# Compressing the sample's cached rows by three block products per pair of blocks instead of four

## What is computed

```python
def _compress(kv, pe, w1, w2):
    # block i covers positions [i*16, i*16 + 32); pe (2, 32, 64); w1 (2, 32, 64, 128); w2 (2, 128, 64)
    ch = kv[:, :n * CMP_STRIDE].reshape(B, n, CMP_STRIDE, 2, K, Dh)
    parts = []
    for half in range(r):                       # r = 2
        sl = slice(half * CMP_STRIDE, (half + 1) * CMP_STRIDE)
        pe_h = jnp.moveaxis(pe[:, sl], 0, 1)[:, :, None]
        proj = jnp.einsum('bncskd,scdh->bnskh', ch + pe_h, w1[:, sl])
        parts.append(proj[:, half:half + n_cmp])
    hid = jax.nn.silu(sum(parts))
    return jnp.einsum('bnskh,shd->bnskd', hid, w2)
```

## Time and profile before

| | us |
|---|---|
| median of 3 runs | 2289.65 (2289.12 to 2290.79) |
| the profiled execution | 2288.92 |
| its span, first to last instruction | 2287.1 |

### The profile page before, as it was taken

One profiled execution on the slowest core, in us unless ns is written; L12 is line 12 of the kernel. 1 busy time (PEld: TensorE's weight loads), 2 busy tenths in 40 slices (PEclk: granted clock), 3 DMA queues, 4 the chain that ended last, 5 costly groups with the idle time before them and its releaser, 6 DMA issues.

```text
span 2287.1 us, 42944 instructions
## 1 busy us (share of the span) xinstructions
PE 2191.5 (96%) x13416; PEld 1569.2 (69%) x13416; DVE 893.4 (39%) x2336; ACT 564.1 (25%) x1372; POOL 646.6 (28%) x733
## 2 busy tenths in 40 slices
PE   7999998999999999999999999989999999999997
PEld 4545567677777777777745556767777677777776
DVE  2013763433453222336510147533344523133475
ACT  2111661211113322120211146411111233121202
POOL 0001771101143334434200037510113334333440
PEclk9999999999999999999999999999999999999999
DMA  9733026999964444544275310389999444444441
GB/s 347 255 148 92 7 78 190 277 277 276 274 231 167 172 172 182 198 190 183 106 276 202 141 61 0 105 264 278 275 284 301 179 155 188 172 172 172 177 166 42
DMA packets 130750, 424.93 MB, mean 186 GB/s; under 512 B 18337, under 2 KB 90274, under 8 KB 114082
## 3 DMA queue, kind: packets, MB, share of 16 engines
q1 hardware_dynamic: 108928, 326.01, 40.2%
q10 hardware_dynamic: 21666, 97.06, 14.6%
HBM read 412.40 MB, written 152.57 MB: 247 GB/s over the span
## 4 chain that ended last, share of the span: by engine, by line
PE 86%; issue 4%; DVE 4%; SPq 1%; POOL 1%; DMA 1%; ACT 1%; DVEq 0%; POOLq 0%; ACTq 0%
PE bank L1099 39%; PE bank L1182 14%; PE bank L1395 10%; PE bank L1568 2%; PE bank L1362 2%; PE bank L1330 2%; PE bank L1342 2%; PE bank L1464 2%; PE bank L1195 1%; PE bank L1592 1%; POOL zone L945 1%; PE bank L1519 1%; DMA ring<-in_cache_kv_cmp 1%; PE bank L1540 1%; SPq L514 1%
## 5 line engine op out<-in xcount | busy, mean ns | idle before, releaser
L1099 PE MATMUL bank<-zone,ring 128*128 128x288 f32 x1664 | 424.8, 407 | 10.3 <-DVE zone L1730 7.6
L1099 PEld LDWEIGHTS bank<-zone,ring 128*128 128x128 f32 x1664 | 314.8, 190 | 103.3 <-DVE zone L1730 13.1
L1099 PE MATMUL bank<-zone,w 128*128 128x288 f32 x1408 | 353.5, 406 | 0.0
L1182 PE MATMUL bank<-ring,hT 128*128 128x512 f32 (+2 forms) x800 | 329.7, 566 | 6.2 <-ACTq L767 4.9
L1099 PEld LDWEIGHTS bank<-zone,w 128*128 128x128 f32 x1408 | 267.5, 190 | 73.9
L1182 PEld LDWEIGHTS bank<-ring,hT 128*128 128x128 f32 (+1 forms) x800 | 147.4, 189 | 157.6 <-issue 146.6
L1395 PE MATMUL bank<-ring,w 128*128 128x128 f32 x2048 | 245.2, 279 | 10.4 <-DMA ring<-in_cache_kv_cmp 10.4
L899 POOL TENSOR_TENSOR w<-ring 128x512 f32<-128x512 f32 x72 | 93.5, 1299 | 546.3 <-PE bank L1099 309.3
L1395 PEld LDWEIGHTS bank<-ring,w 128*128 128x128 f32 x2048 | 235.5, 194 | 14.6 <-DMA ring<-in_cache_kv_cmp 10.5
L629 ACT COPY zone<-bank 128x288 f32<-128x288 f32 x72 | 28.6, 398 | 557.5 <-PE bank L1099 557.5
L1021 POOL TENSOR_TENSOR zone<-constants,stat 128x1024 f32<-128x1024 f32 x16 | 30.3, 1897 | 427.2 <-DVE stat L2089 427.2
(11 more groups left out here) (251 smaller groups left out, 2681.1 us busy)
## 6 DMA issues: line engine op xcount, KB each, us to landing
out_dil_s<-in_state_kv_dil SPq DMA_DIRECT2D x48, 2720.0 KB, 12.3
ring<-in_w_units SPq DMA_DIRECT2D x72, 1024.0 KB, 4.8
ring<-in_cache_kv_cmp SPq DMA_DIRECT2D x256, 128.0 KB, 3.1
ring<-in_cache_kv_sel SPq DMA_DIRECT2D x256, 128.0 KB, 9.9
zone<-in_batch_rows ACTq DMA_DIRECT2D x14, 2112.0 KB
zone<-in_batch_rows ACTq DMA_DIRECT2D x30, 768.0 KB, 5.6
ring<-in_w_in SPq DMA_DIRECT2D x10, 2048.0 KB, 8.1
zone<-in_batch_rows ACTq DMA_DIRECT2D x14, 1088.0 KB, 6.3
```

The costliest lines, as they stand in the source:

```text
L1099: last = mm(dst[:, 0:HALF], lhs[:, k, :], rhs(k), start=first and k == 0, stop=(k == 3), skip_group_check=True)
L1182: last = mm(dst, hT[:, k, t * P:t * P + ROWS[t]], ring[:, n % 2, k * CH:k * CH + width], start=start and k == 0, stop=stop and k == KT - 1)
```

## The change

Neighbouring chunks are treated in pairs, an even one e and an odd one o. Three products are made of each pair in place of four: B·e (`second_of_even`), A·o (`first_of_odd`), and (A + B)·(e + o) (`both_of_sum`). Token e, which is A·e + B·o, is the third less the other two; token o is A·o plus B of the next even chunk. Each of them is 8 products for each s, with 128 columns (64 pairs, 2 heads), so 48 products and 96 MATMUL instructions per sequence in place of 128. The rows in `in_cache_kv_cmp` are laid out for it on the host, with pages of the same size.

New beside them: GpSimd adds the halves of the weights once in a layer (`w1_sum`, 2048 columns) and the pairs of each sequence in place (`add_pairs`, two instructions of 1024 columns, each behind `second_of_even` of its s); ScalarE copies B·e out of its bank (`keep_second`, two copies of 128 columns); VectorE makes the sums (`odd_sums`, `even_sums`: three instructions of 128 columns per s) before exp is taken, now from `summed`. TensorE's window scores wait for the sums, and the compressed values for `h_done` 2. ScalarE issues the window's rows earlier, ahead of the exp of the selected scores.

```diff
-HID_BANK, FIRST_HID = (4, 5), (2, 3)
+HID_BANK, FIRST_HID = (4, 5, 7), (2, 3, 1)
+            def keep_second(it, at):
+                act.wait_ge(h_second.sem, h_second.at(it, 2))
+                for s in range(2):
+                    last = copy(by_page(second[:, s, :, 0:64]), by_head(bank[at][:, s * P:(s + 1) * P]))
+                last.then_inc(h_kept.sem, 1)
...
-                        act.wait_ge(h_full.sem, h_full.at(it, s + 1))
-                        act.wait_ge(h_done.sem, h_done.at(it, s))
-                        nc.scalar.activation(
-                            he.rearrange("p (k n) -> p k n", k=2),
-                            bank[at[s]][:, 0:258].rearrange("p (k n) -> p k n", k=2)[:, :, 1:129],
-                            ACT.Exp, scale=-1.0, bias=ncbias[:, s:s + 1]).then_inc(s_hexp.sem, 1)
+                        act.wait_ge(h_sum.sem, h_sum.at(it, s + 1))
+                        nc.scalar.activation(hes[s].rearrange("p (k n) -> p k n", k=2), summed[:, s], ACT.Exp, scale=-1.0,
+                                             bias=ncbias[:, s:s + 1]).then_inc(s_hexp.sem, 1)
...
+                    if more:
+                        act.wait_ge(win_pv.sem, win_pv.at(it, 1))
+                        load_window(act, l, b + 1)
                     act.wait_ge(s_pad.sem, s_pad.at(it, 1))
                     act.wait_ge(s_max.sem, s_max.at(it, 2))
                     probs(s_sel, 4, slice(0, P))
...
                         load_last_v(act, l, b + 1)
-                        load_window(act, l, b + 1)
...
+                        nc.gpsimd.tensor_tensor(w1_sum, w1[:, :, 0:8, :], w1[:, :, 8:16, :], ALU.add).then_inc(w1_add.sem, 1)
...
+                def add_pairs(it):
+                    for s in range(2):
+                        pool.wait_ge(h_second.sem, h_second.at(it, s + 1))
+                        pool.sem_inc(waits_taken_pool, 1)
+                        nc.gpsimd.tensor_tensor(rawt[:, :, s, :, 0, :], rawt[:, :, s, :, 0, :], rawt[:, :, s, :, 1, :],
+                                                ALU.add).then_inc(raw_sum.sem, 1)
+                add_pairs(l * NB)
                 pool.wait_ge(og_d.sem, og_d.at(l, ROUNDS))
...
                     pad(it + 1)
+                    pool.wait_ge(s_pad.sem, s_pad.at(it + 1, 1))
+                    add_pairs(it + 1)
                     new_keys(it + 1, b + 1)
...
+            def both_of_sum(it, s, at):
+                out = bank[at[2 * s]][:, 2 * P:3 * P]
+                if s == 0:
+                    pe.wait_ge(h_kept.sem, h_kept.at(it, 1))
+                pe.wait_ge(raw_sum.sem, raw_sum.at(it, s + 1))
+                for j in range(8):
+                    last = mm(out, w1_sum[:, s, j, :], rawt[:, :, s, j, 0, :], start=(s == 1 and j == 0), stop=(j == 7),
+                              skip_group_check=True)
+                last.then_inc(h_full.sem, 1)
...
-                        compress(0, 0, 3, HID_BANK[0])
+                        second_of_even(0, HID_BANK)
...
-                        compress(0, 3, 11, HID_BANK[0])
+                        second_of_even(1, HID_BANK)
+                        first_of_odd(0, HID_BANK)
...
-                        compress(0, 11, 16, HID_BANK[0])
-                        compress(1, 0, 16, HID_BANK[1])
-
-                compress(1, 8, 16, FIRST_HID[1])
+                        first_of_odd(1, HID_BANK)
+                        both_of_sum(it + 1, 0, HID_BANK)
+                        both_of_sum(it + 1, 1, HID_BANK)
...
+                    def odd_sums(s):
+                        y = summed[:, s].rearrange("p k (g m e) -> p k g m e", m=4, e=2)
+                        first = by_head(bank[at[1]][:, s * P:(s + 1) * P])
+                        V.tensor_tensor(y[:, :, :, :, 0], first, by_page(second[:, s, :, 0:64]), ALU.add).then_inc(horder.sem, 1)
+                        V.tensor_tensor(y[:, :, :, :, 1], first, by_page(second[:, s, :, 1:65]), ALU.add)
+                        return horder.next()
+                    def even_sums(s, added):
+                        y = summed[:, s].rearrange("p k (g m e) -> p k g m e", m=4, e=2)[:, :, :, :, 0]
+                        dve.wait_ge(h_full.sem, h_full.at(it, s + 1))
+                        V.tensor_tensor(y, by_head(bank[at[2 * s]][:, 2 * P:3 * P]), y, ALU.subtract).then_inc(h_sum.sem, 1)
...
+                    dve.wait_ge(h_kept.sem, h_kept.at(it, 1))
+                    dve.wait_ge(h_first.sem, h_first.at(it, 2))
+                    added = odd_sums(0)
+                    even_sums(0, added)
+                    added = odd_sums(1)
+                    inverse(0)
+                    even_sums(1, added)
+                    keep(0)
+                    inverse(1)
+                    keep(1)
```

More of the change, by code:

```diff
@@ L290, in build, with by_page, by_head @@
         ptd = part(stg_at + 1344, 3, P)
+        at_sums = 6656 + KA + KB
+        second = part(at_sums, 2, 2, 65)
+        summed = part(at_sums + 260, 2, 2, P)
+        hes = [he, part(stg_at + 1728, 256)]
+        assert at_sums + 772 <= W and stg_at + 1984 <= 21900
+        def by_page(v):
+            return v.rearrange("p k (g m) -> p k g m", m=4)
+        def by_head(v):
+            return v.rearrange("p (g k m) -> p k g m", k=2, m=4)
         gb, gm = part(m + 2496, 192, rows=low), part(m + 2048, 192)
@@ L1387, in chunk_outputs, with second_of_even, first_of_odd @@
                 mm(bank[6][:], vcp[:], p_ptc, start=False, stop=True, skip_group_check=True)
-            def compress(s, lo, hi, at):
-                out = bank[at][:, 0:258].rearrange("p (k n) -> p k n", k=2)
-                for j in range(lo, hi):
-                    first = 1 if j < 8 else 0
-                    for k in range(2):
-                        last = mm(out[:, k, first:first + P], w1[:, s, j, :], rawt[:, :, s, k, j % 8, :],
-                                  start=(j == 0 and k == 0), stop=(j == 15 and k == 1), skip_group_check=True)
-                if hi == 16:
-                    last.then_inc(h_full.sem, 1)
+            def second_of_even(s, at):
+                out = bank[at[0]][:, s * P:(s + 1) * P]
+                for j in range(8):
+                    last = mm(out, w1[:, s, 8 + j, :], rawt[:, :, s, j, 0, :], start=(s == 0 and j == 0), stop=(j == 7),
+                              skip_group_check=True)
+                last.then_inc(h_second.sem, 1)
+            def first_of_odd(s, at):
+                out = bank[at[1]][:, s * P:(s + 1) * P]
+                for j in range(8):
+                    last = mm(out, w1[:, s, j, :], rawt[:, :, s, j, 1, :], start=(s == 0 and j == 0), stop=(j == 7),
+                              skip_group_check=True)
+                last.then_inc(h_first.sem, 1)
+            def both_of_sum(it, s, at):
[3 more added lines that the diff above has]
+                pe.wait_ge(raw_sum.sem, raw_sum.at(it, s + 1))
+                pe.sem_inc(waits_taken_pe, 1)
+                for j in range(8):
+                    last = mm(out, w1_sum[:, s, j, :], rawt[:, :, s, j, 0, :], start=(s == 1 and j == 0), stop=(j == 7),
+                              skip_group_check=True)
+                last.then_inc(h_full.sem, 1)
             def prompt_steps(l, g, first, last, ends):
@@ L1422, in prompt_steps @@
                     if ends and m == STEPS:
-                        compress(0, 4, 8, FIRST_HID[0])
+                        second_of_even(1, FIRST_HID)
                     if ends and m == STEPS + 1:
-                        compress(0, 12, 16, FIRST_HID[0])
+                        first_of_odd(1, FIRST_HID)
                     if ends and m == STEPS + 2:
-                        compress(1, 4, 8, FIRST_HID[1])
+                        both_of_sum(l * NB, 1, FIRST_HID)
                     if m == 10:
@@ L1496, in batch @@
                     pe.wait_ge(win_ld.sem, win_ld.at(it, 1))
-                    pe.wait_ge(h_done.sem, h_done.at(it, 2))
+                    pe.wait_ge(h_sum.sem, h_sum.at(it, 2))
                     pe.sem_inc(waits_taken_pe, 1)
@@ L1500, in batch @@
                         sc_full.sem, 1)
+                    pe.wait_ge(h_done.sem, h_done.at(it, 2))
+                    pe.sem_inc(waits_taken_pe, 1)
                     B = bank[SC_BANK[SC_VC]]
@@ L2146, in batch @@
                         raise ValueError((order.k, lay.k))
+                V.memset(second[:, :, :, 64:65].rearrange("p s k o -> p (s k) o"), 0.0).then_inc(h_pad.sem, 1)
+                dve.wait_ge(h_pad.sem, h_pad.at(l, 1))
+                dve.sem_inc(waits_taken_dve, 1)
                 hidden_batch(l * NB, FIRST_HID)
```

61 lines of the change are left out of this document (38 added, 23 removed).

## The result

The changed kernel takes 2271.85 us (median of 4 runs, 2270.14 to 2278.07) against 2289.39 (2289.12 to 2290.79) beside it on the same chip: a ratio of 0.9927, interval 0.9908 to 0.9946. It is 17.5 us faster where 30 were forecast, inside the range of 2248 to 2274. The profiled execution is the slowest of the four, 2278.07 us; its span is 2276.2 us.

What follows compares the result with a forecast made beforehand. TensorE, busy 2191.5 of 2287.1 us, was taken as the bound. 14 x (3.6 removed - 1.3 at the hand-over) = 32.2, less 2 for raw rows, gave 30.2 us gained: 2259 us, range 2248 to 2274.

Steps and rivals of the forecast that it cites:

- What it removes: TensorE, each sequence: 32 of 128 instructions go, 3.6 us (3.76 by merged lengths), in full for 14 sequences.
- The chain: Hand-over between sequences: VectorE and ScalarE steps end later, first score 1.3 us later, one 1.5 us TensorE idle at L1509.
- The bound of 2.0: Upper bound in us of the hand-over loss, if two waits cost 0.36 us instead of 0.04.
- rival (b): TensorE's clock falls in each sequence after the new idle time: 14 x 1.65 = 23 us lost, 2282; chance 0.05.
- Sequence 0: First sequence of each layer: gains nothing, 4.6 us idle ahead; raw rows' wait grows 2 us in all, bounds 0 and 4.
- they take 1.9 us: Window's rows of sequence 1, 512 KB issued between raw pages, at 278 GB/s; 1 us per layer charged.
- The loads: Selected pages at L1519: slack 1 to 2 us, way 2.3 us shorter; zero cost, bounds 0 and 1.3 per sequence.
- GpSimd: Adds of 1024 columns take 2.6 us each, upper bound 6.8, and `w1_sum` 5.2 us in idle time; no cost.
- Rival (c): GpSimd adds in runs of 8 cost 6.8 us each, TensorE waits at `both_of_sum`: 2308; chance 0.05.
- (d): TensorE's products don't get shorter, three costing what four did: 20 us lost, 2310; chance 0.03.
- (e): Hand-over steps cost nothing, other waits having room: 14 x 3.6 = 50 us gained, 2239; chance 0.05.
- Rival (a): DMA becomes the bound, 34.7 us of packets per period: 17.6 us gained, 2272; chance 0.09.

Runs made afterwards that it cites:

- the two kernels with fewer values: Changed kernel with six of eleven dilated-value tiles not loaded: 2269.77 us; the same with reciprocals left out but for 8 of 256 columns: 2243.17 us.
- the three kernels with the early sum: Changed kernel with half 0's even sum earlier: 2261.21 us; page numbers early too: 2253.36; dilated values in 4 KB packets as well: 2245.33.
- the first trace: Profiled execution of the changed kernel in its first measurement, no further edit: 2278.07 us, the slowest of four runs.
- the repeat: The changed kernel run again with no edit: 2275.77 us (6 runs), ratio 0.9943 to the kernel before.

## Why the prediction was right, and where its sizes were off

**What it removes:** right, 3.6 us a sequence: 3.60 on the timeline behind L1571, and 3.60 in the period once neither chain nor loads stood in the way. Busy time fell by 3.76, the other number in the prediction; 0.16 of it turned into idle time of its own.

**The chain:** the mechanism, its place and VectorE as its end were right. The term was mis-sized: 1.78 us against 1.3, by the first score, by L1571 and by the two kernels with fewer values alike, and in three waits rather than one of 1.5 (idle time grew by 1.98, of which 0.2 is busy time turned idle). The sums took 0.29 us, as estimated from the earlier trace rows, and the steps between VectorE and ScalarE 0.03, as good as the 0.04 taken from the earlier trace rows. What the step left out stands ahead of the two even sums: the first started at 401.20, 0.25 us behind the end of its products (T - 1.62), the second at 404.39, 0.24 us behind the end of the reciprocal at 404.15, where 0.04 was taken for each. Besides, exp took 0.51, not 0.47, and half 1's stuck out beyond the first product. So the chain ended at T + 5.28 and not T + 4.9, and the score came 0.16 us later, at T + 5.45 and not T + 5.0. Both stand behind two waits and a semaphore increment in VectorE's list; which of these takes the 0.2 us more is not shown. The bound of 2.0, two waits much longer than 0.04, had been worked out for such a case. This costs 14 x 0.5 = 7 us, the largest error.

**Clock, rival (b):** partly true. Its price of 14 falls did not come, but 3 did, which the sum had put at nothing. In 3 of 14 sequences the granted clock fell to half (1.2 GHz) 0.5 to 1.4 us behind the end of the third wait, here with TensorE's selected scores in it:

```profile
512.83 0.46 PE L1571 MATMUL bank<-zone,gs 64*128 64x128 f32 x2 [1.01 <-DVE gs L2166]
513.12 0.22 PE L1574 MATMUL bank<-c_ident,zone 64*128 64x64 f32 x1
513.32 3.09 PE L1581 MATMUL bank<-ring,q_s 128*64 128x512 f32 x8
```
```profile
513.96:517.37 3.41, 3.41 (x35) 1.55 (x36) 2.06 (x12) 0.86 (x2) 0.20 (x1) 0.50 1.07 349
```

The eight products took 3.09 us instead of 1.94, and the sequence 1.6 more than its neighbours; together 4.7 us. No single idle time reached the 1.5 us that the earlier trace rows had as harmless; three smaller ones stood close together. Over the six traces with the three waits the clock fell at this place in 18 of 84 sequences, and in the three of the kernel before, with and without an edit, in none of 42. In the three kernels with the early sum, which have one wait of 0.7 to 0.8 us there, it fell in 1 of 42, behind a wait for a transfer as well.

**Sequence 0:** the gap ahead of it was 4.55 us, forecast 4.6. The wait for raw rows was the weak term: 2 us in all for the window's rows between the raw pages, bounds 0 and 4. In the first trace the last page landed 4.1 and 1.5 us later relative to the start; in the repeat 1.9 and 13.7. What failed is "they take 1.9 us": bytes divided by a rate, where the last raw page's packets wait on others of another size. The move alone cost the kernel before 13 us; undone in the changed kernel it gave nothing back, as the waits for dilated keys came instead.

**The loads:** right. The selected pages kept 1.3 to 2.3 us of slack, as the window's move gave back what the shorter way took; undone, it left 0.2 to 0.9.

**GpSimd:** right. 2.33 us an add against 2.6, nobody waited for one, and `w1_sum` fell into idle time. Rival (c) is out. So is (d), by the busy time. (e), a chain at no cost, is out by the three waits; its 32.5 us came only with the reciprocals taken away. Rival (a) was right that a floor is near, and wrong in its place: 34.1, not 34.7, and not binding in the changed kernel.

**The sum again,** by measured terms: 14 x 1.78 = 24.9, less 4.7 for the clock, less 5.6 for raw rows and 1.9 at the start gives 12.7; the profiled execution gained 10.9, and the other 1.8 likely lie in more slow clock in sequence 0 (13.1 and 10.2 us at half speed against 6.8 and 6.8) and in periods some tenths longer. The median gained 17.5, with a shorter wait for raw rows and an earlier start in most runs, by what the spread of the repeats suggests; no median execution was traced. That the median lies in the range is in part luck: it is 2 us under the upper end, and the median of the repeat, 2275.77, is 2 us above it. Four errors of one sign, the chain, the clock, the raw rows and the start, took the profiled execution from 30 to 11.

## What to carry to other kernels

Before work is taken off the bounding engine at a hand-over, write out the dependent engine's queue in order and ask which of its steps is queued behind a long one that it doesn't need; here a sum behind a reciprocal cost 1.4 us a sequence and was mended by another order and one more bank. Take a hand-over from the end of one step to the start of the next, not from the bracket of idle time, and look for a row of the same kind for each step: a sum behind two waits came 0.25 us behind what released it, not 0.04. A transfer next to another queue's is not costed by its bytes: look at the packet sizes of both. And when two bounds lie close, take both away in one run before either is believed.

## What the runs showed of the hardware

- Packets of unequal size on two queues: the last raw page's packets of 1 KB went one behind each 22.5-KB packet of the other queue, 1.5 to 1.8 us apart, and the page landed 20 us after its issue. The wait for raw rows in a layer went from 5 to 17 us between executions of one kernel. With the dilated values in rows of 4 KB in place of 22.5 the period went from 34.1 to 32.9 us at the same order of work, and a busy period's rate from about 296 to between 299 and 312 GB/s.
- The clock fell behind idle times of 0.74, 0.42 and 1.01 us within 7.1 us, in 3 of 14 like cases (18 of 84 over all kernels that have them), and cost 1.6 us each time; what sets these apart from the others is open. Once, behind waits of 0.73 us for VectorE and 1.10 us for a transfer, the clock stayed at half for 13.7 us although TensorE had 10.0 us of work in the 10 us from 1640 on, and the period was 40.2 us.
- VectorE and ScalarE handed over in 0.03 us, from the end of one step to the start of the next (402.04 to 402.07); a sum of VectorE behind two waits came 0.24 us behind the reciprocal (404.15 to 404.39), where the reciprocal itself came 0.04 us behind the add.
- GpSimd adds 1024 columns in runs of 8 in 2.33 us, 2.28 ns each; the contiguous add of 2048 for `w1_sum` took 4.50 us, 2.20 ns each, and one of 512 takes 2.54 ns each. The runs cost next to nothing.
